# Norm factor moved to the gate half, last activations split elsewhere, squares summed on GpSimd, four output halves turned ahead

## What is computed

```python
def swiglu(h, w_gate, w_up, w_down):
    return (jax.nn.silu(h @ w_gate) * (h @ w_up)) @ w_down

xp = xp + swiglu(rmsnorm(xp, norm_ffn_g[l]), w_ffn_gate[l], w_ffn_up[l], w_ffn_down[l])
...
y_prompt = rmsnorm(xp, norm_final_g)
y_sample = rmsnorm(xs, norm_final_g)
```

## Time and profile before

| | |
|---|---|
| device time, median of 3 runs | 1979.49 us (1978.79 to 1979.55) |
| device time of the profiled execution | 1979.52 us |
| its span | 1977.7 us |
| PE busy | 1891.5 us, 96% of the span |
| DVE busy | 1043.5 us, 53% |
| ACT busy | 443.2 us, 22% |
| POOL busy | 507.5 us, 26% |

### The profile page before, as it was taken

How to read it: one execution, slowest core, us unless ns; L and a number is a source line. 1 busy time by engine, 2 the same in 40 slices (tenths; PEclk the granted TensorE clock), 3 DMA queues, 4 the chain that set the end, 5 groups by cost and what they waited for, 6 DMA issues and landing times.

```text
span 1977.7 us, 33152 instructions
## 1 busy us (share of the span) xinstructions
PE 1891.5 (96%) x13253; PEld 1751.7 (89%) x13253; DVE 1043.5 (53%) x2108; ACT 443.2 (22%) x902; POOL 507.5 (26%) x371
## 2 busy tenths in 40 slices
PE   6999989999999999999999999999999999999987
PEld 6999987667767899998659999999999999999987
DVE  6698716666676455312553554544544454454455
ACT  5000114555555422101430220000000000000005
POOL 2332222010100145442002223333333333333320
PEclk9999999999999999999999999999999999999998
DMA  4399967586766512225431142342342342211102
GB/s 154 131 311 326 338 214 224 183 248 216 215 189 210 187 54 65 75 76 174 146 107 35 46 164 85 128 169 85 127 170 85 130 176 106 106 42 42 42 21 91
DMA packets 220002, 281.36 MB, mean 142 GB/s; under 512 B 7521, under 2 KB 206569, under 8 KB 218153
## 3 DMA queue, kind: packets, MB, share of 16 engines
q1 hardware_dynamic: 219901, 279.94, 43.4%
HBM read 266.48 MB, written 113.89 MB: 192 GB/s over the span
## 4 chain that ended last, share of the span: by engine, by line
PE 79%; DVE 9%; ACT 3%; SPq 3%; issue 2%; DMA 2%; POOL 1%; DVEq 0%; POOLq 0%; ACTq 0%
PE bank L1543 26%; PE bank L1579 12%; PE bank L1310 8%; PE bank L1071 7%; PE bank L1327 4%; PE bank L1018 3%; PE bank L1189 2%; DVE sp L2165 2%; PE bank L1290 2%; DMA w_raw<-in_w_in_dram 2%; SPq L650 2%; ACT p_T L1700 2%; PE bank L1162 2%; PE bank L1172 1%; PE bank L1505 1%
## 5 line engine op out<-in xcount | busy, mean ns | idle before, releaser
L923 POOL CAST w_hi<-w_raw 128x1024 fp32r<-128x1024 f32 x98 | 103.5, 1057 | 964.1 <-issue 313.7
L1543 PE MATMUL bank<-g_lo,w_hi 128*128 128x362 f32 (+1 forms) x1008 | 333.2, 331 | 0.0
L1543 PE MATMUL bank<-g_hi,w_lo 128*128 128x362 f32 (+1 forms) x1008 | 333.1, 330 | 0.0
L1543 PE MATMUL bank<-g_hi,w_hi 128*128 128x362 f32 (+1 forms) x1008 | 330.5, 328 | 0.0
L925 POOL TENSOR_TENSOR w_lo<-w_raw,w_hi 128x1024 fp32r<-128x1024 f32 x98 | 265.6, 2711 | 7.8
L2573 DVE TENSOR_TENSOR xT<-bank,xT 128x362 f32<-128x362 f32 (+1 forms) x264 | 139.8, 534 | 115.3 <-PE bank L1579 115.3
L1579 PE MATMUL bank<-act_hi,w_hi 128*128 128x364 f32 (+1 forms) x528 | 175.9, 333 | 16.2 <-DVE xT L2573 10.2
L1543 PEld LDWEIGHTS bank<-g_hi,w_lo 128*128 128x128 f32 x1008 | 191.0, 189 | 0.0
L1543 PEld LDWEIGHTS bank<-g_hi,w_hi 128*128 128x128 f32 x1008 | 189.7, 188 | 0.3 <-POOL w_lo L925 0.3
L1543 PEld LDWEIGHTS bank<-g_lo,w_hi 128*128 128x128 f32 x1008 | 189.6, 188 | 0.0
L1579 PE MATMUL bank<-act_lo,w_hi 128*128 128x364 f32 (+1 forms) x528 | 173.9, 329 | 0.0
(11 more groups left out here) (294 smaller groups left out, 3759.9 us busy)
## 6 DMA issues: line engine op xcount, KB each, us to landing
out_sk_dram<-in_cache_win_k_dram SPq DMA_DIRECT2D x24, 2040.0 KB
out_sv_dram<-in_cache_win_v_dram SPq DMA_DIRECT2D x24, 2040.0 KB
kb<-in_cache_win_k_dram SPq DMA_DIRECT2D x48, 512.0 KB, 4.9
vn<-in_cache_win_v_dram SPq DMA_DIRECT2D x22, 1024.0 KB, 7.9
w_raw<-in_w_in_dram SPq DMA_DIRECT2D x22, 512.0 KB, 11.0
w_raw<-in_w_ffn_gate_dram SPq DMA_DIRECT2D x22, 512.0 KB, 3.8
w_raw<-in_w_ffn_up_dram SPq DMA_DIRECT2D x22, 512.0 KB, 3.8
w_raw<-in_w_ffn_down_dram SPq DMA_DIRECT2D x22, 512.0 KB, 3.7
```

The lines of the kernel that those rows point to most:

```text
L923: pool.tensor_copy(w_hi[slot][:, :], w_raw[slot][:, :]).then_inc(w_hi_done, 1)
L1543: last = pe.matmul(out, w, r, start=start, stop=stop)
```

## The change

Five things are changed.

- The multiplication by `factor` moves from after the up results of a chunk to before them: DVE multiplies `gated` by `factor` when the three silu pieces are there.
- The last turn's parts (turn 10) no longer go to `act_hi` and `act_lo` but to the first two chunks of `g_hi` and `g_lo` (`last_hi`, `last_lo`), the normed input, which PE no longer reads once gate and up of turn 10 are through. ACT writes `last_hi` when all of `gated` is there; POOL, instead of DVE, writes `last_lo`. Down of turn 10 reads these.
- Of the eight additions to `acc`, POOL makes the first seven, after it has split the last two weight slices. DVE makes the last one.
- PE turns the first half of token tiles 0 to 3 into banks 0 to 3 right after down of turn 10, ahead of `norm_sums`. Later first halves rotate through banks 0 to 3, second halves through banks 4 to 6.
- To write the above, the loops of ACT and DVE run nine times instead of ten with the last turn written out, and POOL's loop ends one round earlier.

```diff
+        last_hi, last_lo = g_hi[:, 0:2, :], g_lo[:, 0:2, :]
...
-            with pool.Fori(N_XO // 2 + 1, N_SLICES // 2 + 1) as use:
+            with pool.Fori(N_XO // 2 + 1, N_SLICES // 2) as use:
                 for slot in range(2):
                     split(slot, use, more=len(M_TILES[2::3]))
+
+            for ch in range(2):
+                pool.wait_ge(f_hi, 2 * FFT - 1 + ch)
+                pool.tensor_tensor(last_lo[:, ch, :], gated[:, ch, :], last_hi[:, ch, :].bitcast(F32), ALU.subtract)\
+                    .then_inc(f_lo, 1)
+            for slot in range(2):
+                split(slot, N_SLICES // 2, more=len(M_TILES[2::3]))
+
+            for k in range(KC - 1):
+                pool.wait_ge(r_squared, 2 * KC + k + 1)
+                pool.wait_ge(r_summed, 2 * (KC + 1) + k + 1)
+                pool.tensor_tensor(tools_f["acc"][:, :], tools_f["acc"][:, :], tools_f["sq"][k % 2][:, :], ALU.add)\
+                    .then_inc(r_summed, 1)
...
-            down(N_FFN + 6 * FFT - 2)
-
+            down(N_FFN + 6 * FFT - 2, None, last_hi, last_lo)
+
+            def turn_y(t, j):
+                n = P if t < QT else TS
+                if j == 0 and t >= 4:
+                    pe.wait_ge(y_done[0], t - 3)
+                elif j == 1 and t >= 3:
+                    pe.wait_ge(y_done[1], t - 2)
+                out = bank[4 + t % 3] if j else bank[t % 4]
+                for k in range(4):
+                    last = pe.transpose(out[0:n, k * P:(k + 1) * P], xT[:, 4 * j + k, t * P:t * P + n], ident[:, :])
+                last.then_inc(y_turned[j], 1)
+
+            pe.wait_ge(y_scaled, KC // 2)
+            for t in range(4):
+                turn_y(t, 0)
             pe.wait_ge(d_added, 24 * FFT + 2)
             norm_sums(tools_f, 2)
             pe.wait_ge(y_scaled, KC)
...
+                turn_y(t, 1)
+                if t + 4 <= QT:
+                    turn_y(t + 4, 0)
...
+            act.wait_ge(f_gated, 6 * FFT)
+            for ch in range(2):
+                act.activation(last_hi[:, ch, :], gated[:, ch, :], ACT.Copy).then_inc(f_hi, 1)
...
                                 out = gated[:, ch, t0:t0 + w]
-                                dve.wait_ge(f_silu, at(ev, 6))
+                                if g == 0:
+                                    dve.wait_ge(f_whole, at(first_ch + ch + 1, 2))
...
-                        else:
-                            dve.wait_ge(f_gated, at(3 * (first_ch + ch) + 3, 6))
+                            dve.wait_ge(f_silu, at(3 * (first_ch + ch) + 3, 6))
                             dve.tensor_tensor(gated[:, ch, :], gated[:, ch, :], factor[:, :], ALU.mult)\
                                .then_inc(f_whole, 1)
...
             def add_down(n, i=None):
                 for r in range(24):
-                    if i is None and r % 3 == 2 and r > 3:
-                        sum_squares(r // 3 - 1)
```

More of the change, by code:

```diff
@@ L431, in layer_step @@
         y_scaled = sem("y_scaled")
-        y_turned = sem("y_turned")
+        y_turned = [sem(f"y_turned{i}") for i in range(2)]
         y_done = [sem(f"y_done{i}") for i in range(2)]
@@ L1564, in first_gate_up, with down @@
                             norm_factors(tools_f, 1, FACTOR_BANKS)
-            def down(n, i=None):
+            def down(n, i=None, hi=act_hi, lo=act_lo):
                 r_of = lambda r: (24 * (FFT - 1) + r) if i is None else 24 * i + r
@@ L1596, in _ @@
             pe.wait_ge(y_scaled, KC)
-            out_banks = (bank[0], bank[1], bank[2], bank[6])
             for t in range(QT + 1):
[L1599 to L1606, removed]
+                turn_y(t, 1)
+                if t + 4 <= QT:
+                    turn_y(t + 4, 0)
         @block.scalar
@@ L1914, in act_hi_parts @@
                 for ch in range(2):
-                    act.wait_ge(f_whole, ch + 1 if i is None else 2 * i + (ch + 3))
+                    act.wait_ge(f_gated, 3 * ch + 3 if i is None else 6 * i + (3 * ch + 9))
                     act.activation(act_hi[:, ch, :], gated[:, ch, :], ACT.Copy).then_inc(f_hi, 1)
@@ L1919, in _ @@
             act_hi_parts()
-            with act.Fori(0, FFT - 1) as i:
+            with act.Fori(0, FFT - 2) as i:
                 tanhs(i)
                 act_hi_parts(i)
+            tanhs(FFT - 2)
+            act.wait_ge(f_gated, 6 * FFT)
+            for ch in range(2):
+                act.activation(last_hi[:, ch, :], gated[:, ch, :], ACT.Copy).then_inc(f_hi, 1)
             for k in range(KC):
@@ L1934, in _ @@
                 n = P if t < QT else TS
-                act.wait_ge(y_turned, 2 * t + 1)
+                act.wait_ge(y_turned[0], t + 1)
                 if t == 0:
                     act.wait_ge(n_rinv, 6)
-                act.activation(y_nat[t][0:n, 0:512], (bank[0], bank[2])[t % 2][0:n, :], ACT.Copy,
+                act.activation(y_nat[t][0:n, 0:512], bank[t % 4][0:n, :], ACT.Copy,
                                scale=tools_f["rinv"][0:n, t:t + 1])\
@@ L2577, in _ @@
             rest_parts()
-            with dve.Fori(0, FFT - 1) as i:
+            with dve.Fori(0, FFT - 2) as i:
                 gate(N_FFN + 4, i)
@@ L2581, in _ @@
                 rest_parts(i)
+            gate(N_FFN + 4, FFT - 2)
+            add_down(N_FFN + 8, FFT - 2)
             dve.memset(tools_f["acc"][:, :], 0.0).then_inc(r_summed, 1)
@@ L2588, in _ @@
                 n = P if t < QT else TS
-                dve.wait_ge(y_turned, 2 * t + 2)
-                dve.tensor_scalar(y_nat[t][0:n, 512:D], (bank[1], bank[6])[t % 2][0:n, :],
+                dve.wait_ge(y_turned[1], t + 1)
+                dve.tensor_scalar(y_nat[t][0:n, 512:D], bank[4 + t % 3][0:n, :],
                                   tools_f["rinv"][0:n, t:t + 1], None, ALU.mult)\
```

2 lines of the change are left out of this document (1 added, 1 removed).

## The result

The changed kernel took 1960.26 us (median of 4 runs, 1959.31 to 1964.15) against 1979.52 us (4 runs, 1978.79 to 1983.68): ratio 0.9902, interval 0.9885 to 0.9918. It is 19.3 us faster where 25.1 were forecast, and 1.3 us outside the range. Two later comparisons of the same two kernels gave ratios of 0.987 (0.9849 to 0.9891) and 0.9891 (0.987 to 0.9912).

A forecast was written before the change was run, and what follows sets the result against it. PE, busy 96% of the span, was taken to set the time outside its stalls. Terms of 11.2, 7.6, 3.9 and 2.4 us sum to 25.1 off 1979.52: 1954.4 us, range 1952.0 to 1959.0.

The forecast's parts named there:

- Term A: Down in the loop: moving the factor's pass removes PE's 1.12 us stall at result 2, ten times, 11.2 us.
- The pass costs nothing in the gate half: Behind the three silu pieces: DVE's idle time covers the moved factor pass, so it was costed at nothing.
- Term B: Between down of turns 9 and 10: waiting and slow-clock loss of 8.1 us goes, 0.5 us clearing stall remains; 7.6 us.
- Rival 1: Down of turn 10: POOL falls behind with the squares; price 4.4 us, total 1958.8 us, chance 0.06.
- Rival 5: Down of turn 10: POOL's sums take so long the kernel is slower; at 8 us each, 1989 us; chance 0.02.
- Term C: Down of turn 10: squares on POOL remove six PE stalls and start the last addition 0.65 us sooner; 3.9 us.
- Rival 2: Down of turn 10: DVE's additions are locked out while POOL sums; price 8.3 us, total 1962.7 us, chance 0.04.
- Term D: The end: halves turned ahead save 1.3 us in the norm sums and 1.1 us behind them; 2.4 us.
- Rivals 3 and 4: 3: PE's wait at result 2 moves to another release, up to 11.2 us, chance 0.05; 4: no change, 1979.5, 0.01.

The follow-up runs named there:

- second profile of before: The kernel before, profiled and timed again without an edit; median 1978.91 us (12 runs), ratio 1.0005.
- Factor alone: Only the multiplication by factor moved to the gate half, on the kernel before; 1971.40 us, ratio 0.9954.
- pause put back: Changed kernel with an unused DVE pass ahead of down's additions each turn, where the factor's pass stood; 1966.62 us, ratio 0.9917 to the kernel before.
- last parts alone: Only the last turn's parts moved to g_hi and g_lo, POOL writing the rests, on the kernel before; 1969.90 us, ratio 0.9952.
- squares alone: Only seven of the eight additions of squares moved from DVE to POOL, on the kernel before; 1975.48 us, ratio 0.9978.
- second halves first: Changed kernel, acc cleared ahead of the loop, second halves of tiles 0 to 2 turned before tile 4's first half; ratio 0.9867 to the kernel before.
- PE kept busy: Changed kernel plus 8 unread products behind the 16 blocks and 5 between second and first halves; 1956.22 us, ratio 0.9872 to the kernel before.
- third execution: The changed kernel, unedited, profiled and timed a third time; 1956.71 us, ratio 0.9891 to the kernel before.

## Why the prediction was off

**Term A (11.2 us): the mechanism was right, the size was not.** "So the whole 1.12 us goes, ten times" came true to the letter: down takes 23.94 us in the chain, no gap at result 2. The step that failed is the one from there to the sum, "Bounds: 0 if another wait ended at the same moment, 11.2 if none". It took gate and up as fixed, and they are not: in the kernel before every second turn was 0.37 us shorter, in the first of its four weight slices, five times in all, and those are gone, 1.9 us. The loop gained 9.3 (9.7 against the second profile of before, which had four such turns). The two lengths stood in the chain of before; I had shown only its pieces of down. Factor alone and pause put back show that the shorter slices go and come with the stall. What in PE makes the two lengths, and why only some of the turns behind a stall have the shorter one, stays open; no run here separates it.

**The pass costs nothing in the gate half**: right. It even got shorter: 1.29 us in 21 of its 22 places (3.4 in one of turn 0, which makes the mean 1387 ns), against 1742 ns on average in the kernel before, second profile. In the new place POOL is idle beside those 21; in the old one POOL's CAST and its rest ran beside each pass, and the rest took 3.30 us (from 1893.92) instead of 2.40. PE waits for nothing there.

**Term B (7.6 us): right.** The last parts alone gave 7.7; the clock is 1.00 between the turns (1914 to 1918 and on until 1945.0); one gap of 0.45 us instead of 0.5. The last parts were ready at 1900.05, earlier than the "1907 is nearer" of the prediction. Rival 1 and Rival 5 did not come: POOL took 2.55 us for a sum, 0.02 under the estimate from the rests. (The Trainium skill, "GPSIMD Engine Reference", 3.1 Elementwise, gave an estimate of 2.39: 6% under the trace.)

**Term C (3.9 us): right.** Down of turn 10 lost its six stalls (3.5 or 3.2 us in squares alone, 3.25 forecast); the last addition starts 0.37 us behind the last product's start and ends 0.90 behind it. Rival 2 did not come: DVE's additions stay at 0.54 us beside POOL. The rule of the Trainium skill ("SBUF — State Buffer", SBUF: two separate sides) was not put to the test by the sums: DVE's one sum of the last part starts at 1941.62, behind POOL's last, which ends at 1941.17. The factor's pass above, with its two SBUF inputs, bears on it, and the rows agree: the pass took 0.45 us more beside POOL and POOL's rest 0.90 more, about what each had left of the other's work when it started.

**Term D (2.4 us): too large, by about 1.** Its first half was right in this pair: norm sums of 2.17 us, 1.7 saved against 1.3 forecast (0.9 on average over all executions). Its second half, the "1.1 saved" behind the sums, came to nothing: from the end of the sums to the end of the span 17.1 us pass before and after. The step that failed is "so the end moves with the first tiles". Tile 0 did come sooner, though less than "tile 0 is done at 1.5 us instead of 2.8" (DVE's half starts 1.2 us behind the sums and ends at 1.9), but tile 1 did not. Tile 1 came 2.39 us behind tile 0 (0.8 with second halves first), for two reasons that the prediction did not have: PE's order puts the first half of tile 4, which waits for ACT, ahead of tile 1's second half; and the clock fell behind the sums to 0.50, while the prediction priced the clock only in the sums. Second halves first takes away the first reason (1.5 us). PE kept busy takes away the second in one of its two executions (0.9 to 2.0 us behind the last product), and there tile 1 still came 1.93 us late, so the order counts without the clock. The whole end gained 2.3 us, the last addition's 0.65 among it, so D is about 1.6 in this pair. It is uncertain by 1 us: two executions of the kernel before ended 25.1 and 23.8 us behind the last product, by when in the end the clock fell and came back.

**The part ahead.** The sum was taken "off the profiled execution's 1979.52", with everything ahead of the loop as it was. In the fourteen profiled executions, all with the same code ahead, the loop's start lay between 1155.5 and 1167.5 us. So of the 5.8 us between forecast and result, 2.8 are the terms above (1.9 in A, 0.8 in D with C's end, 0.1 elsewhere), and the rest, 3.0, I put down to this spread, though only the profiled runs show where they lost time: by the three comparisons the change gained 19.3, 25.0 and 22.4 us. The range had no term for it, because the three times of before given with the profile lay within 0.8 us of each other; later runs of the same kernel spread over 15.4. With 22.3 us for the region the forecast would have been 1957.2, in its range. So the shortfall of 2.8 us in the terms is an error of the prediction, but that the total fell outside the range was chance as well: the medians of the two later comparisons, 1954.85 and 1956.71, lie inside it. Rivals 3 and 4 did not come.

## What to carry to other kernels

When a regular stall is taken out of a loop, compare the lengths of all stages of a turn, turn by turn, before multiplying: the stage behind a stall may take another time for it. At an end made of tiles, follow the first three or four tiles through PE's order of issue, the releases it waits for and the clock, since the first tile alone moves nothing. And give the untouched part of a long program a spread of its own in the range: three equal runs are no proof that there is none.

## What the runs showed that I had not expected

- The first 72 products of one and the same stage took 11.73 or 12.11 us at a granted clock of 1.00, while the 216 behind them always took the same. In the loop the shorter time came only in turns behind a stall of 1.1 us, and there only in some.
- The granted clock of the changed kernel was 0.50 from 1945.0 on, behind 1.44 us without work and 18 products of one column, and stayed there until 1951.8 while PE was busy (3.80 of 3.80 us from 1948). In its third execution, with the same code, it was low at this place for half as long, 3.4 us against 6.8.
- The kernel before took 1970.3 to 1985.7 us in 65 runs, and profiled executions part at many stages ahead, in waits for weights and in the clock.
